# A fused two-block transformer kernel: the four gate projections of block one's merged attention as its first units, with the silu taken at their evacuation

## The reference

```
q_l = apply_axial_rope(qk_heads(q_l), rope)
k_l = apply_axial_rope(qk_heads(k_l), rope)
s = einsum('bqhjd,bkhjd->bhjqk', q, k) * scale
p = softmax(s)
attn = p[:, :, 0] - lam * p[:, :, 1]
o = einsum('bhqk,bkhe->bqhe', attn, v)
out = rms_norm(o, subln_g) * (1.0 - lam_init) * silu(z)
```

## Time and profile before

| | |
|---|---|
| median of 3 runs | 2997.34 us (2997.01 to 3000.13) |
| the profiled execution, its own time | 2998.88 us |
| its span, first to last instruction | 2997.1 us |
| mean granted PE clock | 0.928 of full |
| PE busy over the span | 2592.3 us (86%) |
| DVE, ACT, POOL busy | 1407.2, 936.9, 206.8 us |
| attention of layer one, first matmul to the last DVE instruction | from about 232 to 474 us |
| attention of layer two, the same | from about 1036 to 1241 us |

### The profile page before, as it was taken

The page is one execution under the profiler, slowest core; times in us unless marked ns, Lnnn a source line. Parts: engine busy times, 40 slices in busy tenths (PEclk is TensorE's granted clock), DMA queues, the critical chain, the costliest instruction groups (busy, mean ns, idle before and its releaser), DMA issues. The chain is left out here.

```text
span 2997.1 us, 47694 instructions
## 1 busy us (share of the span) xinstructions
PE 2592.3 (86%) x19606; PEld 1990.4 (66%) x19606; DVE 1407.2 (47%) x2317; ACT 936.9 (31%) x1510; POOL 206.8 (7%) x347
## 2 busy tenths in 40 slices
PE   5899998868868899895987799889999897899997
PEld 1277667658846666665885566558878565588885
DVE  1145551356663555336665666453332464533323
ACT  0233442211123344321112555442222345422221
POOL 0000000055200000005520000000000000000000
PEclk9989999789979899877998999899999998999998
DMA  8431111100001211110001212113333221133332
GB/s 323 118 72 50 29 36 49 32 2 3 3 15 43 68 46 36 50 46 2 3 3 43 77 57 63 43 56 98 98 90 96 85 67 57 57 97 98 96 91 72
DMA packets 300767, 185.10 MB, mean 62 GB/s; under 512 B 5650, under 2 KB 284708, under 8 KB 300460
## 3 DMA queue, kind: packets, MB, share of 16 engines
q1 hardware_dynamic: 293580, 166.79, 18.6%
q0 software_dynamic: 1808, 5.26, 1.1%
q10 hardware_dynamic: 5200, 10.49, 1.0%
HBM read 177.79 MB, written 4.71 MB: 61 GB/s over the span
## 5 line engine op out<-in xcount | busy, mean ns | idle before, releaser
L243 DVE TENSOR_TENSOR wlo<-wraw,whi 128x1024 fp32r<-128x1024 f32 (+1 forms) x276 | 333.5, 1208 | 598.6 <-ACT whi L236 597.6
L280 PE MATMUL PW<-hhi,whi 128*128 128x512 f32 (+1 forms) x1184 | 448.5, 379 | 65.3 <-DVE hlo L761 39.2
L281 PE MATMUL PW<-hhi,wlo 128*128 128x512 f32 (+1 forms) x1184 | 445.3, 376 | 0.0
L282 PE MATMUL PW<-hlo,whi 128*128 128x512 f32 (+1 forms) x1184 | 444.4, 375 | 0.0
L236 ACT ACTIVATE whi<-wraw 128x1024 fp32r<-128x1024 f32 (+1 forms) x276 | 288.3, 1045 | 313.7 <-PE PW L282 289.7
L280 PEld LDWEIGHTS PW<-hhi,whi 128*128 128x128 f32 x1184 | 225.9, 191 | 115.9 <-issue 49.7
L335 PE MATMUL PW<-hhi,whi 128*128 128x512 f32 (+1 forms) x640 | 242.8, 379 | 23.4 <-DVE hlo L734 18.8
L282 PEld LDWEIGHTS PW<-hlo,whi 128*128 128x128 f32 x1184 | 225.9, 191 | 40.3
L281 PEld LDWEIGHTS PW<-hhi,wlo 128*128 128x128 f32 x1184 | 226.3, 191 | 38.5
L337 PE MATMUL PW<-hlo,whi 128*128 128x512 f32 (+1 forms) x640 | 226.9, 355 | 0.0
L336 PE MATMUL PW<-hhi,wlo 128*128 128x512 f32 (+1 forms) x640 | 226.9, 355 | 0.0
(11 more groups left out here) (376 smaller groups left out, 4583.9 us busy)
## 6 DMA issues: line engine op xcount, KB each, us to landing
wraw<-in_w_in SPq DMA_DIRECT2D x68, 512.0 KB, 3.9
wraw<-in_ffn_w_gate SPq DMA_DIRECT2D x44, 512.0 KB, 3.8
wraw<-in_ffn_w_up SPq DMA_DIRECT2D x44, 512.0 KB, 3.8
wraw<-in_ffn_w_down SPq DMA_DIRECT2D x32, 512.0 KB, 3.7
mod_w<-in_mod_w SPq DMA_DIRECT2D x7, 2048.0 KB, 8.1
wraw<-in_attn_w_in SPq DMA_DIRECT2D x24, 512.0 KB, 3.7
mod_w<-in_mod_w ACTq DMA_DIRECT2D x5, 2048.0 KB, 19.8
wraw<-in_w_out SPq DMA_DIRECT2D x16, 512.0 KB, 3.7
```

Source lines behind the costliest of these rows:

```text
L243: dve.tensor_tensor(wlo[:, slot, 0:kb, :], wraw[:, slot, 0:kb, :], whi[:, slot, 0:kb, :].bitcast(F32), ALU.subtract).then_inc(S("w_split"), 1)
L280: pe.matmul(acc, whi[:, u % 2, k, :], rhi[:, k0 + k, s0:s1], start=a, stop=False)
L281: pe.matmul(acc, wlo[:, u % 2, k, :], rhi[:, k0 + k, s0:s1], start=False, stop=False)
L282: last_mm = pe.matmul(acc, whi[:, u % 2, k, :], rlo[:, k0 + k, s0:s1], start=False, stop=b)
```

## The change

The four z units go to the front of the list of units, before head 0's q, k and v, so every index into the q, k, v units grows by 4. All seven units are run before slot 0 (less the last three chunks, which stand beside the first scores). Nothing is left to spread over head 3's slots, and the closing "unit" entry, at which the last segment is copied out, moves ahead of head 3's first slot. The z segments are evacuated with Silu instead of Copy; the silu in place after the last slot is gone, and DVE waits for the evacuations instead. The table set of Exp and Ln is loaded at slot 0 and not at the phase's start.

```diff
-                return lambda a, s0, s1, acc: a.activation(dest[:, h, s0:s1], acc, ACT.Copy)
+                return lambda a, s0, s1, acc: a.activation(dest[:, h, s0:s1], acc, ACT.Silu)
...
             for h in range(4):
+                units.append(dict(w=w, k0=0, kb=8, col=C_AZ + P * h, segs=SEGS[n], evac=put(z, h)))
+            for h in range(4):
                 for j, (dest, c0, m) in enumerate(((q, C_AQ, n), (k, C_AK, TOK), (vch, C_AV, TOK))):
...
-            for h in range(4):
-                units.append(dict(w=w, k0=0, kb=8, col=C_AZ + P * h, segs=SEGS[n], evac=put(z, h)))
...
-            done = sum(dense.chunks(u) for u in range(3))
+            done = sum(dense.chunks(u) for u in range(7))
             lead = done
             for h in range(4):
-                nxt = range(3 * (h + 1), 3 * (h + 2)) if h < 3 else range(12, 16)
+                nxt = range(4 + 3 * (h + 1), 4 + 3 * (h + 2)) if h < 3 else range(0)
...
             for s in range(ns + 4):
+                if s == 3 * HS:
+                    order.append(("unit", c, 0))
                 order.append(("first", s, 0))
...
-            order.append(("unit", c, 0))
...
             def act_program(a):
-                a.preload_act_table_set("natural_log_exp_and_others")
...
                     elif name == "first":
+                        if i == 0:
+                            a.preload_act_table_set("natural_log_exp_and_others")
...
-                for h in range(4):
-                    evacuated(a, 12 + h)
-                    a.activation(z[:, h, 0:n], z[:, h, 0:n], ACT.Silu).then_inc(S("attn_silu"), 1)
...
                 for h in range(4):
-                    v.wait_ge(S("attn_silu"), 4 * l + h + 1)
+                    evacuated(v, h)
                     v.tensor_tensor(mix[:, 4 + h, 0:n], mix[:, 4 + h, 0:n], z[:, h, 0:n], ALU.mult)
```

More of the change, by code:

```diff
@@ L907, in pe_scores @@
                     e.wait_ge(roped.sem, roped.at(2 * h + 2))
-                    evacuated(e, 3 * h)
-                    evacuated(e, 3 * h + 1)
+                    evacuated(e, 4 + 3 * h)
+                    evacuated(e, 4 + 3 * h + 1)
                 if i:
@@ L937, in pe_vturn @@
                 if half == 0:
-                    evacuated(e, 3 * h + 2)
+                    evacuated(e, 4 + 3 * h + 2)
                 if half or h:
@@ L1041, in dve_rope @@
                 x = (q, k)[which][:, h % 2, 0:SEQ]
-                v.wait_ge(*dense.evacuated(3 * h + which))
+                v.wait_ge(*dense.evacuated(4 + 3 * h + which))
                 v.stream_shuffle(rot[:, 0, :], x, [j ^ 16 for j in range(32)])
@@ L1072, in attention @@
             c = 0
-            for u in range(12):
-                if u % 3 < 2:
-                    at_chunk[c + 9 if u else 9] = ("rope", u // 3, u % 3)
+            for u in range(16):
+                if u >= 4 and (u - 4) % 3 < 2:
+                    at_chunk[c + 9] = ("rope", (u - 4) // 3, (u - 4) % 3)
                 c += dense.chunks(u)
```

## The result

The changed kernel takes **3021.19 us**, median of 4 runs (3019.04 to 3026.62), where the kernel before, beside it, takes 2997.69 (2997.01 to 3000.13). The ratio is 1.008, with a 95% interval of 1.0062 to 1.0097. The profiled execution has 3020.19 us, 21.3 more than that of before.

What follows compares the result with a forecast made beforehand. Head 3 was taken as bound by PE, filled by z chunks; without them by waits through PE, DVE and ACT. 33.4 - 19.5 + 21.8 - 16.0 = +19.7, plus 5 for the clock: +24.7, forecast 3022 us, range 3011 to 3033.

Steps and rivals of the forecast that it cites:

- its ring: Softmax chain of a slot: scores on PE, maxima on DVE, exponentials on ACT, combine on DVE, each waiting for the last.
- Added at the front: Four z units ahead of head 0's slots, at PE's pace: +33.4 us in layer one, +21.8 in layer two.
- Layer one's slots: Head 3 without chunks, slots 18 to 22: 6.7, 5.5, 6.9, 5.5 and 3.7 us, together 28.3.
- Layer two's slots: Head 3 without chunks, slots 12 to 15: 5.1, 7.2, 7.6 and 5.5 us, together 25.4 where 39.7 stood before.
- The tail: Layer two, from the last turn to the end of normed: 15.25 us as before, then the product, 2.5.
- The clock: PE's clock falls about halfway through layer one's head 3 (values 2.9, two slots 2.4 less overlap), none more in layer two: +5 us.
- clock low all through head 3: Rival: low clock in head 3 of both layers, only the values matmul lifting it; +32 to +36, about 3031 us; chance 0.20.
- clock holds: Rival: short gaps in head 3 never suffice for a fall of PE's clock; +19.7, 3017 us; chance 0.25.
- Table loads: ACT's loads ahead of the first exponentials and in the rwkv projections are hidden, cost nothing; without cover 1.28 us each.
- a faster ring: Rival: head 3's wide slots overlap more, below about 3.5 us each; at 3.3 us the kernel takes 2995; chance 0.02.
- an ideal overlap: Rival: head 3's wide slots last only DVE's 4.2 us, giving about 8 of the 19.7; 3009 to 3012 us; chance 0.03.
- doesn't do what it says: Rival: the chunks still stand in head 3, only the products' wait for the silu goes; 2994 us; chance 0.02.

## Why the prediction was right, and where it wasn't

The forecast was 3022 with slower at 0.96; 3021.19 was measured. The mechanism is confirmed by the kernel without z: the units cost their full time in front, and head 3 gives back only what stood above its ring. The nearness of the number is partly luck: the sum for the two attentions was +24.7 and they took +27.3 (layer one 18.9 forecast and 18.1 measured, layer two 5.8 and 9.3), and 6 us came back elsewhere.

- *Added at the front.* +33.4 and +21.8 forecast. Head 3's first turn came 443.19 - 409.46 - 0.72 = 33.0 later in layer one, and 1221.29 - 1182.01 - 17.73 = 21.55 in layer two (17.73 is how much later its first evacuation comes, 1059.34 - 1041.61). Right.
- *Layer one's slots.* Forecast 6.7, 5.5, 6.9, 5.5, 3.7; measured 6.69, 5.45, 6.69, 5.79, 4.14. Right but for the last two, at the lower clock.
- *Layer two's slots.* Forecast 5.1, 7.2, 7.6, 5.5; measured 5.14, **10.54**, 7.38, 5.93. Slot 13 is the step that failed. The prediction took "turn, values, a small turn, scores" from PE's order, and leaves out that the copy of slot 12's probabilities waits for these values on ACT, with the next exponentials queued behind it. The scores wait for the exponentials, so values and exponentials add instead of overlapping. With the exponentials first the slot fell to 8.72, so this queue was 1.8 of the missing 3.3; for the other 1.5 the rows have PE's small turn, which waits 0.84 for the copy behind the values, and values that last 5.32 and not 4.8 (read, not tested). Slot 13 is most of the 3.4 us by which layer two came out above its +5.8.
- *The tail.* From the last turn to the product 15.25 forecast, 15.33 measured in layer two.
- *The clock.* +5 forecast, all in layer one: head 3 and its tail took 49.7 where 45.1 stood for full clock, so at most +4.6. The fall came halfway, in slot 20, as I had put it. The split was off: values 1.9 (forecast 2.9), slots 0.7 (forecast about 2.1, what is left of the 5) and the small matmuls of the tail 1.6, which I had at nothing. A wide slot at the lower clock cost 0.3 (slot 21, 5.79 against 5.45) and not the 1.2 of my price: eight scores took 2.43 and not 2.9, and lie in part under the combine. The +5 is thus right as a sum and not in its terms. In layer two I expected none more: its values took 7.71 where before they had 8.18, nearly the same price, and slot 15 lost 0.4. The rival "clock low all through head 3" falls by the row at 443 to 458 us, with PE 53% busy at 1.00; "clock holds" by the one behind it.
- *The page's rule on transposes* ("TensorE: Matmul & The Clock Gate", "Part 4: PE-mode transpose" in the Trainium skill) would have the clock fall early in head 3 of both layers. It held for 15 us in layer one and 21 in layer two, and fell later; the trace agrees with the rule only in part.
- *Table loads.* Hidden, as forecast, in front and in the projections (at 546.85 and 563.53 us, 1.28 each; ACT still waits 5.28 us for PE behind each, and the units keep their pace). The silu's half as a whole gives 3.1 us against four units with a late silu. In my sum it was the 1.94 and 1.68 of waiting taken out of the tails: right.
- *Not forecast at all:* the -6 us in projections and scan of layer two. My sum assumed that untouched stages keep their length; in these traces they keep it within 7 us.
- The rivals of a faster ring and of an ideal overlap fall by the 5.45 us of a plain slot; "doesn't do what it says" by the rows of the front.

## What to carry to other kernels

Work that fills another chain's waits has two prices: nothing where it stands, its full time anywhere else, and how much of it is free is read by subtracting the ring's slot from the slot as it is, not from the busy share. Before moving it away, look for where waits are still uncovered: here the tail behind the last softmax, where 8 chunks of each layer won 9.6 us in the two attentions, 2.8 of them by a higher granted clock at layer two's last values. And when a slot is summed from one engine's order, follow each wait through the queue of the engine that is waited for: exponentials queued behind a copy that waits for a matmul cost 1.8 us in one slot and some 5 in a layer.

## What the runs showed that I had not expected

Stages with the same instructions took 226.8 to 233.7 us (scan 2, at a mean granted clock of 0.94 down to 0.91) and 251.5 to 255.1 (scan 1, 0.91 down to 0.89). The kernel with one z unit in front, whose attentions cost 0.5 us more than before, had a median 5 us below it (2992.34 against 2997.57); its trace puts the gain in the scans. A difference of less than about 7 us between two versions of this kernel needs the stage by stage table before it is given a cause.

TensorE kept 2.4 GHz (granted clock 1.00) from 443 to 458 us while busy 7.90 of 15 us with scores and turns, and dropped to 1.2 in the slots behind, whose matmuls are of the same kinds (13.55 of 18 us busy at the lower clock, the start of the values included).
